# Eight more early expert tiles, two to a batch in the last eight routing batches

## The chip, the cores and the metric

The kernel runs on one core of a Trainium2 chip. The metric is the device time of one execution in microseconds (us); lower is better. A core has a matrix engine (TensorE, PE in the profile, with its weight loads as PEld), a vector engine (VectorE, DVE), a scalar engine (ScalarE, ACT), a general one (GpSimd, POOL) and one that here only issues transfers (SyncE, SP). Each engine works through its own list of instructions in order; semaphores tie the lists together.

## The reference

One transformer layer on 512 tokens of width 1024: a mixer (windowed attention beside a gated delta rule), then a PEER layer. In PEER every token picks, in each of 8 heads, 16 of 16,384 experts, by top-k over two lists of 128 sub-keys; each expert is one row of a table u and one of a table v:

```
out = einsum('tk,tkd->td', gelu(einsum('tkd,td->tk', u_tab[idx], x)) * gate, v_tab[idx])
```

## The kernel before

Tokens come in four blocks of 128. For blocks 1 to 3 (384 tokens) PEER is computed densely: the 16,384 experts form 128 tiles of 128 experts. "Up" multiplies a tile of u with the 384 tokens (24 matmuls of 128x384, since every operand is split into a high and a low part and three products are summed over 8 slices of the width), gelu follows, then a gate matrix that is zero where an expert was not picked, then "down" with the tile of v (18 matmuls of 128x512). For block 0 PEER is computed sparsely by "pairs": 128 picks, for each of which POOL gathers one row of u and v for every token (1 MB a gather, six slots), VectorE does one "dot" (L1528) and one "add" (L1545), and ScalarE a small gelu for each four dots (L1533). 128 dots and 128 adds are 256 steps of VectorE; `pair_steps` hands them out over the places of a list of rates, in groups of four dots, then four adds.

`routing` comes before `experts`. It picks the experts on VectorE and builds the gate matrix for the blocks b = 1, 2, 3, each in 16 batches k of 8 tokens. In a batch VectorE writes two one-hot tiles, oi (`first_keys`, one batch ahead) and oj; ScalarE scales oi to og (`gated`, eight instructions, L1798); TensorE multiplies og with oj (the products, L1762); ScalarE copies them out (L1814), and SP stores 1 MB of gates for each two batches. As TensorE has little to do there, routing also does the up step of some tiles ahead of time, the early tiles: 24 before the first batch and one in each of the 48 batches. An early tile n needs: a load of u by SP into one of four buffers; `split_u(n)` on ScalarE (L1776); `u_low(n)` on VectorE (L1665); the 24 matmuls of `up(n)` (L1734 to L1736); `gelu(n)` on ScalarE (L1783) into a single buffer, which is stored to memory (L1788, 192 KB) and read back in `experts`. `gelu(n)` waits until the store of n-1 has landed, and on ScalarE `split_u(n + 2)` stands right behind `gelu(n)`:

```
for n in early(b, k): gelu(n)        # evict(b, k): gelu(n), split_u(n + 2), store of n
```

In the order of the engines, for batch k of block 3:

- VectorE: oi(k+1), oj(k), `u_low` of the early tiles of batch k+1, the pair steps of batch k
- ScalarE: `gated(k)`, the pair gelu of the dots of batch k-1, `evict(k-1)` (the early tiles' gelu, split and store, then the copies of the products)
- TensorE: `up` of the early tiles of batch k, the products of batch k
- SP: the loads of u for the tiles four ahead, and after each odd batch a store of gates, which waits for `evict(k)`
- POOL: gathers for the pairs, as many as routing has dots; gather j waits for add j-6

`experts` then runs over the 128 tiles: the first NMT = 56 with both up and down, the other 72 with down alone, with the stored gelus. Its steps of the pairs go at 2.7 a tile in the first part and 1.0 in the second.

Of the kernel before, what the change touches and what calls it, by code (L numbers as in the profile page):

```python
# [12 lines left out]
P = 128  # L13
# [27 lines left out]
NK = 128  # L41
# [7 lines left out]
GT = 4  # L49
NG = NK // GT  # L50

EARLY = 72
NU = 4
TD = T - P
GRP4 = 4
# [1202 lines left out]
def output_projection(nc, m, ps, sem, w_out_in, early_u_in, u_t, norm_ffn_g, w_q, keys, h_dram):  # L1258
# [35 lines left out]
    with ExitStack() as ctx:  # L1294
# [14 lines left out]
        with nc.Block() as block:  # L1309
            @block.sync  # L1310
            def _(sp):
# [6 lines left out]
                for i in range(2):  # L1318
                    sp.dma_start(m.u_raw[i], u_t[NK - EARLY + i]).then_inc(early_u_in[i], 16)

# [237 lines left out]
def pair_steps(rates):  # L1558


    todo = [(what, GRP4 * g + i) for g in range(HA // GRP4) for what in ("dot", "add") for i in range(GRP4)]
    places, at, due = [], 0, 0.0
    for rate in rates:
        due += rate
        here = []
        while at < len(todo) and due >= 1.0:
            what, k = todo[at]
            if what == "add" and k % GRP4 == 0 and ("dot", k + GRP4 - 1) in here:
                break
            here.append(todo[at])  # L1570
            at, due = at + 1, due - 1.0
        places.append(here)
    places[-1] = places[-1] + todo[at:]
    return places


def routing(nc, m, ps, sem, u_in, next_u, u_t, gates, gelus, pairs_of_0, steps):
# [13 lines left out]
    NBT = P // BT  # L1591
    RING = 3
    ST = 16
    FIRST = 24
    AFTER = [()] + [tuple(range(NBT))] * (TB - 1)
    assert FIRST + sum(len(v) for v in AFTER) == EARLY

    def early(b, k):

        if b < 0:  # L1600
            return range(FIRST)
        n = FIRST + sum(len(v) for v in AFTER[:b]) + sum(i < k for i in AFTER[b])
        return range(n, n + (k in AFTER[b]))

    SMALL_AT = NBT - 2

    for n in early(-1, 0):
        banks.add(("up", n), "act")
    banks.add(("small", 1), "dve")
    for b in range(1, TB):  # L1610
        for k in range(NBT):
            for n in early(b, k):
                banks.add(("up", n), "act")
            for i in range(BT // 4):
                banks.add(("G", b, k, i), "act")
            if k == SMALL_AT and b + 1 < TB:
                banks.add(("small", b + 1), "dve")

    with ExitStack() as ctx:
# [47 lines left out]
        def slot(b, k):  # L1667
            return (NBT * (b - 1) + k) % RING

        def wait_products(eng, b, k):  # L1670

            n = NBT * (b - 1) + k - RING
            if n >= 0:
                banks.wait_full(eng, ("G", n // NBT + 1, n % NBT, BT // 4 - 1))

        with nc.Block() as block:
            @block.sync
            def _(sp):
                def load_u(n):

                    if n >= NU:
                        sp.wait_ge(u_lo, n - NU + 1)
                    sp.dma_start(u_raw[n % NU], u_t[NK - EARLY + n]).then_inc(u_in[n % NU], 16)

                for n in range(2, FIRST + NU):
                    load_u(n)
                for b in range(1, TB):
                    for k in range(NBT):
                        for n in early(b, k):
                            if n + NU < EARLY:  # L1690
                                load_u(n + NU)
                            else:
                                i = n + NU - EARLY
                                sp.wait_ge(u_lo, n + 1)
                                sp.dma_start(u_raw[i], u_t[i]).then_inc(next_u[i], 16)
                        if (k + 1) * BT % ST == 0:
                            q = ((k + 1) * BT // ST - 1) % 2
                            banks.wait_taken(sp, ("G", b, k, BT // 4 - 1))
                            t0 = (b - 1) * P + (k + 1) * BT - ST
                            sp.dma_start(gates[:, :, t0:t0 + ST, :].rearrange("g i t j -> i g (t j)"),  # L1700
                                         stage[:, q].rearrange("p g t j -> p g (t j)")).then_inc(stored[q], 16)
                for half in range(2):
                    sp.wait_ge(stored[half], 16 * (TD // ST // 2))
                sp.wait_ge(ge_out, 16 * EARLY)

# [63 lines left out]
            @block.scalar  # L1769
            def _(act):  # L1770
                def split_u(n):
                    act.wait_ge(u_in[n % NU], 16 * (n // NU + 1))
                    if n >= 2:

                        banks.wait_full(act, ("up", n - 2))
                    nc.scalar.activation(uh[:, n % 2, :], u_raw[n % NU], ACT.Copy).then_inc(u_hi, 1)  # L1776

                def gelu(n):

                    banks.wait_full(act, ("up", n))  # L1780
                    if n:
                        act.wait_ge(ge_out, 16 * n)
                    nc.scalar.activation(ge[:], banks.bank(("up", n))[:, 0:TD],  # L1783
                                         ACT.Gelu).then_inc(banks.taken["act"], 1)
                    if n + 2 < EARLY:
                        split_u(n + 2)
                    banks.wait_taken(act, ("up", n))
                    act.dma_start(gelus[n], ge[:]).then_inc(ge_out, 16)  # L1788

                def exps(b):  # L1790
                    act.wait_ge(subbed, b + 1)
                    nc.scalar.activation(best[:], best[:], ACT.Exp).then_inc(exped, 1)

                def gated(b, k):
                    act.wait_ge(oi_ready, NBT * (b - 1) + k + 1)
                    wait_products(act, b, k)
                    for t in range(BT):
                        ins = nc.scalar.activation(og[:, slot(b, k), t, :], oi[:, slot(b, k), t, :], ACT.Copy,  # L1798
                                                   scale=smallT[:, b % 2, 1, k * BT + t:k * BT + t + 1])
                        if t % 4 == 3:  # L1800
                            ins.then_inc(og_ready, 1)

                def evict(b, k):
                    for n in early(b, k):
                        gelu(n)
                    for i in range(BT // 4):
                        g = ("G", b, k, i)
                        banks.wait_full(act, g)
                        at = k * BT + 4 * i
                        half, q = (at // ST) % 2, (b - 1) * (P // ST) + at // ST  # L1810
                        if q >= 2 and at % ST == 0:
                            act.wait_ge(stored[half], 16 * (q // 2))
                        t0 = at % ST
                        nc.scalar.activation(stage[:, half, :, t0:t0 + 4, :].rearrange("p g t j -> p t g j"),  # L1814
                                             banks.bank(g)[:].rearrange("p (t g j) -> p t g j", t=4, j=GJ),
                                             ACT.Copy).then_inc(banks.taken["act"], 1)

                split_u(0)
                split_u(1)
                for n in early(-1, 0):  # L1820
                    gelu(n)
                    if n in (9, 20):
                        exps(n // 20)
                for b in range(1, TB):
                    for k in range(NBT):
                        gated(b, k)
                        if b == TB - 1 and k:
                            pairs_of_0.scalar_steps(act, steps[k - 1])
                        if k:
                            evict(b, k - 1)  # L1830
                        if k == 9 and b + 1 < TB:
                            exps(b + 1)
                    evict(b, NBT - 1)
                pairs_of_0.scalar_steps(act, steps[NBT - 1])
# [389 lines left out]
def hybrid_layer(nc, a, out):  # L2224
# [3 lines left out]
    with ExitStack() as ctx:  # L2228
# [55 lines left out]
        slots = [rows[:, i] for i in range(4)] + [more[:, i] for i in range(2)]  # L2284
        pairs_of_0 = Gathered(nc, sem, slots, m.mix[:, 0, :], mem.take("pair_index", [P, HA], U32)[:],
                              mem.take("pair_gate", [P, HA])[:], a["peer_uv"], mem.take)
        rates = [2.0] * (P // 8) + [2.7] * (NK - EARLY) + [1.0] * EARLY
        steps = pair_steps(rates)
        before, after = steps[:P // 8], steps[P // 8:]
        routing(nc, m, ps, sem, early_u_in, u_in, a["peer_u"], gates, gelus, pairs_of_0, before)  # L2290
        experts(nc, m, ps, sem, u_in, a["peer_u"], a["peer_v"], gates, gelus, h_dram, out, pairs_of_0, before, after)

# [23 lines left out]
```

## Time and profile before

| | us |
|---|---|
| median of 3 runs | 1674.74 |
| these runs | 1674.64 to 1679.88 |
| the profiled execution | 1674.7 |
| its span, first to last instruction | 1672.9 |

| engine | busy us | share of the span |
|---|---|---|
| TensorE | 1567.6 | 94% |
| VectorE | 1305.2 | 78% |
| ScalarE | 713.8 | 43% |
| GpSimd | 340.4 | 20% |

Times of rows count from the start of the span. Block 3 of the routing lies between 776 and 890 us, `experts` from 890 us to the end. In a row of the timeline the first number is the start, the second the duration, and what stands in brackets is the idle time of the engine before it and what ended that.

### The profile page before, as it was taken

How to read it: one execution, taken by the hardware profiler on the slowest of the kernel's cores; microseconds unless marked ns; L12 is line 12 of the kernel's file. 1: busy time of each engine (PE TensorE's matmuls, PEld its weight loads, DVE VectorE, ACT ScalarE, POOL GpSimd, SP SyncE). 2: the span in 40 equal slices, each digit the busy share in tenths (PEclk: the TensorE clock that was granted, in tenths of full speed). 3: DMA queues.
4: the chain of work that ended last, by engine and by line, in shares of the span. 5: the costliest groups of instructions: out<-in, count | busy, mean ns of one | idle time of the engine just before them, and what ended most of it. 6: DMA issues, size and time to landing. Idle time of an engine off the chain costs nothing. (4 is left out here: it accounts for less than half of the span.)

```text
span 1672.9 us, 24431 instructions
## 1 busy us (share of the span) xinstructions
PE 1567.6 (94%) x9241; PEld 1405.8 (84%) x9241; DVE 1305.2 (78%) x2270; ACT 713.8 (43%) x1411; POOL 340.4 (20%) x303
## 2 busy tenths in 40 slices
PE   7999787988899889989996999999999999999998
PEld 6898777767789889889995899999999988888886
DVE  4638775453499799998894988888798888998996
ACT  4645442132233668777672333333333333333331
POOL 5012710000165200020401221222222221100100
PEclk9999887988999999999998999999999999999999
DMA  5220003031144456686988988888898789999992
GB/s 191 76 76 8 2 2 132 22 139 63 56 156 157 148 157 194 205 302 213 358 278 342 407 315 316 324 317 314 323 364 293 275 345 382 368 363 345 352 339 90
DMA packets 147159, 380.89 MB, mean 228 GB/s; under 512 B 10480, under 2 KB 89456, under 8 KB 128368
## 3 DMA queue, kind: packets, MB, share of 16 engines
q1 hardware_dynamic: 118256, 231.17, 39.3%
q0 software_dynamic: 18432, 134.23, 20.6%
q10 hardware_dynamic: 10368, 14.16, 2.3%
q8 instruction: 60, 0.98, 0.2%
q14 instruction: 43, 0.35, 0.1%
HBM read 336.00 MB, written 43.52 MB: 227 GB/s over the span
## 5 line engine op out<-in xcount | busy, mean ns | idle before, releaser
L1521 POOL DMA_INDIRECT scores<-in_peer_uv,pair_index x86 | 123.6, 1437 | 626.6 <-DVE pair_sum L1545 462.7
L2114 PE MATMUL bank<-v_hi,act_hi 128*128 128x512 f32 x552 | 215.2, 390 | 5.0 <-DVE v_lo L2177 5.0
L2116 PE MATMUL bank<-v_hi,act_lo 128*128 128x512 f32 x552 | 219.3, 397 | 0.0
L2115 PE MATMUL bank<-v_lo,act_hi 128*128 128x512 f32 x552 | 216.4, 392 | 0.0
L1734 PE MATMUL bank<-x_hi,early_u_h 128*128 128x384 f32 x576 | 201.1, 349 | 16.3 <-POOL early_u_l L1665 11.5
L1735 PE MATMUL bank<-x_lo,early_u_h 128*128 128x384 f32 x576 | 196.9, 342 | 0.0
L1736 PE MATMUL bank<-x_hi,early_u_l 128*128 128x384 f32 x576 | 196.2, 341 | 0.0
L2190 DVE TENSOR_TENSOR act_tile<-gelu_tile,gate_tiles 128x384 f32<-128x384 f32 x128 | 119.7, 935 | 83.3 <-ACT gelu_tile L2162 71.0
L2102 PE MATMUL bank<-x_hi,u_split 128*128 128x384 f32 x448 | 151.6, 338 | 12.7 <-DVE u_split L2172 12.7
L2104 PE MATMUL bank<-x_hi,u_split 128*128 128x384 f32 x448 | 151.5, 338 | 0.0
L2103 PE MATMUL bank<-x_lo,u_split 128*128 128x384 f32 x448 | 151.5, 338 | 0.0
L1798 ACT ACTIVATE onehot_gated<-onehot_i,rt_smallT 128x128 f32<-128x128 f32 x384 | 117.8, 399 | 34.3 <-DVE onehot_i L1949 34.3
L2150 ACT ACTIVATE act_hi<-act_tile 128x384 fp32r<-128x384 f32 x128 | 66.8, 522 | 142.2 <-DVE act_tile L2190 122.7
L1734 PEld LDWEIGHTS bank<-x_hi,early_u_h 128*128 128x128 f32 x576 | 109.9, 191 | 20.8 <-POOL early_u_l L1665 6.7
L2114 PEld LDWEIGHTS bank<-v_hi,act_hi 128*128 128x128 f32 x552 | 103.8, 188 | 26.8 <-issue 6.2
L2162 ACT ACTIVATE gelu_tile<-bank 128x384 f32<-128x384 f32 x56 | 27.5, 491 | 228.1 <-PE bank L2104 228.0
L2115 PEld LDWEIGHTS bank<-v_lo,act_hi 128*128 128x128 f32 x552 | 103.7, 188 | 23.5
L2116 PEld LDWEIGHTS bank<-v_hi,act_lo 128*128 128x128 f32 x552 | 103.6, 188 | 22.5
L2177 DVE TENSOR_TENSOR v_lo<-v_raw,v_hi 128x1024 fp32r<-128x1024 f32 x92 | 112.3, 1220 | 9.9 <-ACT v_hi L2144 9.9
L2144 ACT ACTIVATE v_hi<-v_raw 128x1024 fp32r<-128x1024 f32 x92 | 96.7, 1051 | 33.8 <-DMA v_raw<-in_peer_v 31.7
L1762 PE MATMUL bank<-onehot_j,onehot_gated 128*128 128x128 f32 x768 | 96.2, 278 | 14.8 <-DVE onehot_j L1949 12.2
L1735 PEld LDWEIGHTS bank<-x_lo,early_u_h 128*128 128x128 f32 x576 | 110.0, 191 | 0.0
(327 smaller groups left out, 3674.7 us busy)
## 6 DMA issues: line engine op xcount, KB each, us to landing
v_raw<-in_peer_v SPq DMA_DIRECT2D x128, 512.0 KB, 6.5
u_raw<-in_peer_u SPq DMA_DIRECT2D x64, 512.0 KB, 6.3
u_raw_more<-in_peer_u SPq DMA_DIRECT2D x64, 512.0 KB, 6.0
gates<-gate_stage SPq DMA_DIRECT2D x24, 1024.0 KB, 5.8
gate_tiles<-gates SPq DMA_DIRECT2D x16, 1536.0 KB, 14.3
early_gelus<-early_gelu ACTq DMA_DIRECT2D x72, 192.0 KB
gelu_tile<-early_gelus SPq DMA_DIRECT2D x72, 192.0 KB, 7.7
w_raw<-in_w_in SPq DMA_DIRECT2D x9, 1024.0 KB, 5.3
```

Of the source, the lines that this page charges most:

```text
L1521: pool.indirect_dma_start(self.slot(k), None, self.table, bass.IndirectOffsetOnAxis(ap=self.sidx[:, k:k + 1], axis=0)).then_inc(self.lande ...
L1734: nc.tensor.matmul(banks.bank(g)[:, 0:TD], uh[:, q, w], m.xh[:, k, P:], start=(k == 0), stop=False)
L1735: nc.tensor.matmul(banks.bank(g)[:, 0:TD], uh[:, q, w], m.xl[:, k, P:], start=False, stop=False)
L1736: t = nc.tensor.matmul(banks.bank(g)[:, 0:TD], ul[:, q, w], m.xh[:, k, P:], start=False, stop=(k == KD - 1))
L1798: ins = nc.scalar.activation(og[:, slot(b, k), t, :], oi[:, slot(b, k), t, :], ACT.Copy, scale=smallT[:, b % 2, 1, k * BT + t:k * BT + t + 1])
L2102: nc.tensor.matmul(bank, uh[:, q, w], m.xh[:, k, P:], start=(k == 0), stop=False)
L2103: nc.tensor.matmul(bank, uh[:, q, w], m.xl[:, k, P:], start=False, stop=False)
L2104: t = nc.tensor.matmul(bank, ul[:, q, w], m.xh[:, k, P:], start=False, stop=(k == KD - 1))
L2114: nc.tensor.matmul(bank[:], ah[:, s, w], v_hi[:, c], start=first, stop=False)
L2115: nc.tensor.matmul(bank[:], ah[:, s, w], v_lo[:, c], start=False, stop=False)
L2116: t = nc.tensor.matmul(bank[:], al[:, s, w], v_hi[:, c], start=False, stop=last)
L2190: nc.vector.tensor_tensor(af[:], ge[:, n % NG2, :], gt[:, it % 2, :, jj], ALU.mult).then_inc(gate_f, 1)
```

## The change

`EARLY` goes from 72 to 80, so NMT goes from 56 to 48. In the batches 8 to 15 of block 3 there are two early tiles instead of one. The pair steps of these batches go from 2 to 4 a batch. On ScalarE `evict(k-1)` now stands ahead of the pair gelu of batch k-1.

```diff
-EARLY = 72
+EARLY = 80
...
     AFTER = [()] + [tuple(range(NBT))] * (TB - 1)
+    AFTER[-1] += tuple(range(NBT // 2, NBT))
...
-        return range(n, n + (k in AFTER[b]))
+        return range(n, n + AFTER[b].count(k))
...
                         gated(b, k)
+                        if k:
+                            evict(b, k - 1)
                         if b == TB - 1 and k:
                             pairs_of_0.scalar_steps(act, steps[k - 1])
-                        if k:
-                            evict(b, k - 1)
...
-        rates = [2.0] * (P // 8) + [2.7] * (NK - EARLY) + [1.0] * EARLY
+        rates = [2.0] * (P // 16) + [4.0] * (P // 16) + [2.7] * (NK - EARLY) + [1.0] * EARLY
```

## Rows read from the trace of the kernel before

**Rows 1.** Two stretches: length; busy PE, PEld, DVE, ACT, POOL; clock; DMA share; GB/s.

```profile
822.00:876.00 54.00, 51.29 (x330) 51.13 (x329) 46.92 (x52) 38.67 (x99) 10.28 (x6) 0.97 0.87 304
930.00:1340.00 410.00, 410.00 (x2070) 371.41 (x2069) 346.18 (x419) 142.86 (x216) 101.07 (x67) 1.00 0.85 323
```

**Rows 2.** The chain that ended last: start, us, what; same instruction, successive tiles.

```profile
954.65 0.24 PE bank L2116
962.98 0.24 PE bank L2116
...
1369.60 0.24 PE bank L2115
1386.19 0.24 PE bank L2115
```

**Rows 3.** Timeline of TensorE in block 3: the products of two successive batches.

```profile
847.96 1.95 PE L1762 MATMUL bank<-onehot_j,onehot_gated 128*128 128x128 f32 x16
...
853.97 1.95 PE L1762 MATMUL bank<-onehot_j,onehot_gated 128*128 128x128 f32 x16
```

**Rows 4.** Timeline of VectorE in block 3.

```profile
797.25 1.22 DVE L1949 TENSOR_TENSOR onehot_i<-rt_iota_row,rt_smallT 128x1024 f32<-128x1024 f32 x1
...
822.00 1.22 DVE L1949 TENSOR_TENSOR onehot_i<-rt_iota_row,rt_smallT 128x1024 f32<-128x1024 f32 x1
...
834.76 1.22 DVE L1665 TENSOR_TENSOR early_u_l<-u_raw,early_u_h 128x1024 fp32r<-128x1024 f32 x1 [4.27 <-ACT early_u_h L1776]
835.91 1.22 DVE L1528 SCALAR_TENSOR_TENSOR scores<-scores,mix 128x1024 f32<-128x1024 f32 x1
...
838.19 1.22 DVE L1949 TENSOR_TENSOR onehot_i<-rt_iota_row,rt_smallT 128x1024 f32<-128x1024 f32 x1
...
848.43 0.15 DVE L1539 TENSOR_TENSOR pair_c<-pair_g,pair_gate 128x4 f32<-128x4 f32 x1
...
851.01 1.22 DVE L1949 TENSOR_TENSOR onehot_i<-rt_iota_row,rt_smallT 128x1024 f32<-128x1024 f32 x1
...
875.94 1.22 DVE L1949 TENSOR_TENSOR onehot_j<-rt_iota_row,rt_smallT 128x1024 f32<-128x1024 f32 x1
```

**Rows 5.** Timeline of ScalarE: stores of early gelus and the gelus behind them.

```profile
536.05 0.33 ACTq L1788 DMA_DIRECT2D early_gelus<-early_gelu  x1
538.22 0.49 ACT L1783 ACTIVATE early_gelu<-bank 128x384 f32<-128x384 f32 x1 [1.25 <-PE bank L1736]
...
796.62 0.33 ACTq L1788 DMA_DIRECT2D early_gelus<-early_gelu  x1
...
798.50 2.47 ACT L1798 ACTIVATE onehot_gated<-onehot_i,rt_smallT 128x128 f32<-128x128 f32 x8
804.91 0.49 ACT L1783 ACTIVATE early_gelu<-bank 128x384 f32<-128x384 f32 x1 [3.95 <-DMA early_gelus<-early_gelu]
...
805.43 0.33 ACTq L1788 DMA_DIRECT2D early_gelus<-early_gelu  x1
...
809.90 0.49 ACT L1783 ACTIVATE early_gelu<-bank 128x384 f32<-128x384 f32 x1 [0.24 <-DMA early_gelus<-early_gelu]
...
823.65 0.33 ACTq L1788 DMA_DIRECT2D early_gelus<-early_gelu  x1
...
833.29 0.49 ACT L1783 ACTIVATE early_gelu<-bank 128x384 f32<-128x384 f32 x1 [5.42 <-DMA early_gelus<-early_gelu]
```

**Rows 6.** The groups by line of instructions: ScalarE's copies of the products, two a batch.

```profile
L1814 ACT ACTIVATE gate_stage<-bank 128x512 f32<-128x512 f32 x96 | 51.5, 592 | 0.9 <-ACT early_gelu L1783 0.9
```

**Rows 7.** Timeline of GpSimd: the last of four gathers.

```profile
829.34 1.96 POOL L1521 DMA_INDIRECT scores<-in_peer_uv,pair_index  x1 [0.30 <-issue]
```

**Rows 8.** Timeline of SP: loads of u, the last store of gates, the first load of experts.

```profile
819.66 3.76 SPq L1683 DMA_DIRECT2D u_raw_more<-in_peer_u  x2
...
884.71 0.38 SPq L1700 DMA_DIRECT2D gates<-gate_stage  x1
890.23 0.33 SPq L2053 DMA_DIRECT2D gate_tiles<-gates  x1
```

## The prediction

> **What bounds the kernel now.** I read the page first (TensorE busy in 94% of the span), then the busy time by stretch, then the chain of waits, then the timelines of TensorE, VectorE, ScalarE and SP around the last eight routing batches. The reader is to see two things. In `experts` TensorE has no idle time at all (410.00 of 410.00 us) [rows 1], and the chain that ended last is TensorE's alone: a tile with up and down takes 962.98 - 954.65 = 8.33 us, one with down alone (1386.19 - 1369.60) / 4 = 4.15 us [rows 2]. In the routing batches into which the tiles move, TensorE is nearly full as well: 51.29 of 54 us [rows 1], one batch each 853.97 - 847.96 = 6.01 us [rows 3]. So the change moves work of the bounding engine from one full stretch to another. What it can win at most is TensorE's idle time there, some 3 us in the stretch; what it can lose is whatever keeps TensorE waiting in the eight changed batches.
>
> **The change part by part.**
>
> *Experts.* Eight tiles lose their up step: 8 x (8.33 - 4.15) = -33.4 us [rows 2]. They gain a read of 192 KB each, and routing a store of as much, 3 MB in all. In experts reads lie under TensorE; if that cover were gone, 1.5 MB at 323 GB/s [rows 1] would be 5 us. The 16 pair steps that leave experts leave VectorE, which has slack there (346 of 410 us busy [rows 1]): nothing. The loads of u are as many as before.
>
> *TensorE in routing.* One up step is 8.33 - 4.15 = 4.18 us, so the products are 6.01 - 4.18 = 1.83 us and a batch with two up steps 10.2 us. Eight of them give the 33.4 us back exactly. If TensorE stayed the bound, the change would be worth nothing either way.
>
> *The handoff between ScalarE and VectorE.* This is where I see the cost. `split_u(n + 2)` stands behind `gelu(n)`. With one tile a batch, two tiles ahead are two batches ahead: `u_low` in VectorE's batch k needs only `evict(k-1)`, which follows `gated(k)`, whose oi was written in the batch before. With two tiles a batch, two tiles ahead are one batch ahead. VectorE's batch k needs `evict(k)`, which on ScalarE follows `gated(k+1)`, which needs oi(k+1), which VectorE writes at the start of that same batch k. So the engines take turns, once round in every batch, and the second `u_low` also waits for the second gelu, which waits for the store of the first to land. All of VectorE's pair steps stand behind that, and oi(k+2) behind them. (The old place of the pair gelu would even close a circle; that is why its move costs nothing but is needed. In the first eight batches it now stands some 1.3 us later, and the adds that wait for it have `u_low` before them.)
>
> The round, from the start of oi:
> - oi to the start of `gated`: 798.50 - 797.25 = 1.25 us; the eight scalings 2.4 us (2.47 in the row, of which the last overlaps) [rows 4, 5]. The first gelu starts at 3.6.
> - first gelu to second gelu: X, below.
> - gelu to `u_low` (through the split): 834.76 - 833.29 = 1.47; `u_low` 835.91 - 834.76 = 1.15 [rows 4, 5].
> - pair steps: two dots take 838.19 - 835.91 = 2.28, so four take 4.6; two adds with the small multiply take 851.01 - 848.43 = 2.58, so four take 5.0 [rows 4].
>
> That is 10.8 + X for a batch of dots and 11.2 + X for one of adds. The rounds are VectorE's batches 8 to 14, four of dots and three of adds: 4 x 10.8 + 3 x 11.2 = 76.8 us plus seven X.
>
> X is 0.5 us from gelu to the issue of its store, then the time until the next gelu may start. No row of before shows two gelus waiting in this way in these batches; the bounds are these [rows 5]. Below: 538.22 - 536.05 = 2.2 us, where the store wasn't what was waited for. Above: 833.29 - 823.65 = 9.6 us, right behind loads of u (issued until 823.4 [rows 8]) and among gathers, the last of them issued until 831.3 [rows 7]. Between: 8.3 us (804.91 - 796.62) and 4.5 us (809.90 - 805.43). In the changed batches the last load of u is released by the `u_low` of the round before, about 9 us ahead of the store, so it should be out of the way. The gathers are not: four follow the adds of batches 9 and 11 and two those of 7 and 13, and they run while the first gelu of batches 10, 12, 8 and 14 is stored. For these four I take 6.0 us, below the middle of 4.5 and 9.6 because the loads are gone; for the three others 2.2. With the 0.5: 4 x 6.5 + 3 x 2.7 = 34.1 us.
>
> The rounds together: 76.8 + 34.1 = 110.9 us, 15.8 a batch, against the 10.2 of TensorE, which now waits.
>
> Batch 7 is half such a round: its second `u_low` needs the gelu that before came at 833.29. VectorE's batch 7 began at 822.00 [rows 4]. If that gelu comes as late as before, it ends at 834.76 + 1.15 + 2.58 = 838.5, 16.5 us; with a short store ScalarE's own work (the store's issue at 823.65, copies of 2 x 0.6 [rows 6], `gated` at 2.5, in all some 4.2 us) puts the gelu near 827.9, `u_low` at 829.4 and the end 3.7 us later, 11.1 us in all. I take 13.8.
>
> Before, the same stretch of VectorE, oi in batch 7 to oj in batch 15, was 875.94 - 822.00 = 53.9 us [rows 4]. So: 110.9 + 13.8 - 53.9 = +70.8 us.
>
> *The end of routing.* From oj(15) to the first load of experts it took 890.23 - 875.94 = 14.3 us, 5.5 of it the last store of gates [rows 4, 8]. With two gelus there it is about 0.3 + X + 0.5 for the gelu + 1.1 for the copies [rows 6] + 0.4 + the same 5.5, so 10.5 at X = 2.7 and 14.3 at X = 6.5: I take -2, and 0 and -4 as ends.
>
> **Sum:** -33.4 + 70.8 - 2 = +35.4 us on 1674.7 us of the profiled execution, which is also the median of the runs: 1710 us.
>
> The Trainium skill speaks against one term, and for the first rival below. The Trainium skill (DMA: Bandwidth & Descriptors, section "Queues, rings and completion order") says that a DMA engine takes turns between the queues that have work. A 192 KB store would then share with two other queues, and at the 304 GB/s of this stretch the 0.38 MB of the others would add some 1.3 us to 2.2; by that estimate the four long waits are 3.5 us, not 6.0, and the time is 10 us shorter, 1700. The 9.6 and 8.3 us that the timeline shows speak against it.
>
> **The rivals.**
> - *Stores land fast even beside gathers.* All X = 2.7, batch 7 at 11.1, the end at -4: 76.8 + 18.9 + 11.1 - 53.9 - 4 - 33.4 = +15.5, so 1690. For it: the 4.5 us beside gathers. Against it: 8.3 and 9.6. This is the low end. 0.12.
> - *Stores land late everywhere*, 9.6 beside gathers and 4.5 elsewhere: 4 x 10.1 + 3 x 5.0 = 55.4; with 16.5 and 0 that is 76.8 + 55.4 + 16.5 - 53.9 - 33.4 = +61.4, so 1736. 0.05.
> - *TensorE falls to the lower of its two clock levels* (1.2 in place of 2.4 GHz), since it now idles some 5 us in a batch, in pieces. At half the clock a batch of TensorE takes up to 2 x 10.2 = 20.4 us, over the 15.8 of the round; if it stayed there for all seven, +32 us, 1742; for half of them 1726. For it: every batch has such gaps. Against it: the mean of 0.97 in this stretch [rows 1] in spite of the wait behind the 9.6 us store, so it came back soon. Short falls cost nothing, as TensorE isn't the bound. 0.08.
> - *The other side: TensorE stays the bound.* If the turns overlap, because some split comes a batch earlier than I read, a batch is 10.2 us, and the two 33.4 cancel. The time is 1669 to 1676, the low end if the 4.27 us stall of VectorE in the stretch [rows 4] goes. It decides as soon as the round is under 10.2 us, which even with X = 0 it isn't by the order of the instructions (10.8). 0.07.
>
> **How the numbers follow.** The forecast has 0.68, with a range of its own of 1697 to 1727. A measurement of this kernel tells about 0.3%, 5 us, from no change. All cases but the last are slower: 0.93; the last gives 0.05 within and 0.02 faster. The range from 1690 to 1733 reaches to the low rival and to a clock that is low for most of the rounds; it leaves out the last rival, the late stores and the edges of the others, under 2 in 10.
>
> **What would show it.** In the changed kernel: `early_u_l` on VectorE waiting for `early_u_h` some 3 us and again X us in each of the batches 8 to 14; the products of these batches 13 to 19 us apart and uneven, longer after batches of adds; TensorE waiting for `early_u_l`; the gelus of second tiles waiting for the store; experts at 8.33 and 4.15 us a tile, 33.4 us shorter. Products 10.2 us apart would prove me wrong on the turns; waits that alternate otherwise, on the stores.

## The result, and the profile after

The changed kernel takes 1721.85 us (median of 4, 1718.95 to 1728.51) against 1675.68 us (median of 4): a ratio of 1.0276, 95% interval 1.0241 to 1.0312. It is slower, 46 us by the medians, where +35 (1710 us) was forecast; 1721.85 lies in the range of 1690 to 1733. The profiled execution took 1718.95 us with a span of 1717.2, 44.3 us more than the 1672.9 of before. One of the eleven runs of e10 below, the profiled one, took 2579.5 us at a mean granted clock of 0.56 where the others took 1661 to 1674, and no reading rests on it. From here on "round" means the time from one oi(k+1) to the next on VectorE, counted by batch k.

First the busy time by stretch of the changed kernel (length; then busy us of PE, PEld, DVE, ACT and POOL, with instructions; granted clock; DMA share; GB/s): the stretch of [rows 1], then rounds 8 and 9 by themselves, then experts.

```profile
822.00:876.00 54.00, 40.27 (x233) 37.94 (x232) 30.21 (x31) 23.62 (x56) 12.79 (x8) 0.94 0.77 268
834.14:854.61 20.47, 13.03 (x68) 12.27 (x67) 9.31 (x12) 6.18 (x14) 2.86 (x2) 0.83 0.78 278
854.61:868.25 13.64, 11.07 (x68) 10.59 (x67) 9.67 (x12) 6.38 (x15) 2.67 (x2) 1.00 0.38 107
1000.00:1300.00 300.00, 299.75 (x1514) 271.35 (x1513) 253.10 (x307) 103.61 (x156) 79.04 (x49) 1.00 0.85 325
```

In experts TensorE is as full as before once it has started. In the routing stretch TensorE is busy 40.27 of 54 us where it was 51.29 [rows 1]. VectorE, 30.21, isn't full either: no engine is. That is what engines look like that take turns. VectorE's timeline shows the turns (start, us, instruction, idle time before it):

```profile
834.14 1.22 DVE L1950 TENSOR_TENSOR onehot_i<-rt_iota_row,rt_smallT 128x1024 f32<-128x1024 f32 x1
...
839.20 1.23 DVE L1666 TENSOR_TENSOR early_u_l<-u_raw_more,early_u_h 128x1024 fp32r<-128x1024 f32 x1 [2.70 <-ACT early_u_h L1777]
848.89 1.22 DVE L1666 TENSOR_TENSOR early_u_l<-u_raw_more,early_u_h 128x1024 fp32r<-128x1024 f32 x1 [8.46 <-ACT early_u_h L1777]
...
854.61 1.22 DVE L1950 TENSOR_TENSOR onehot_i<-rt_iota_row,rt_smallT 128x1024 f32<-128x1024 f32 x1
...
859.66 1.22 DVE L1666 TENSOR_TENSOR early_u_l<-u_raw,early_u_h 128x1024 fp32r<-128x1024 f32 x1 [2.70 <-ACT early_u_h L1777]
862.12 1.23 DVE L1666 TENSOR_TENSOR early_u_l<-u_raw,early_u_h 128x1024 fp32r<-128x1024 f32 x1 [1.23 <-ACT early_u_h L1777]
...
868.25 1.22 DVE L1950 TENSOR_TENSOR onehot_i<-rt_iota_row,rt_smallT 128x1024 f32<-128x1024 f32 x1
...
952.35 1.22 DVE L1950 TENSOR_TENSOR onehot_j<-rt_iota_row,rt_smallT 128x1024 f32<-128x1024 f32 x1
```

Where [rows 4] had one wait of 4.27 us in eight batches (the others of that stretch are 1.1 us or less), each round now has two: 2.70 us for the first split, the same in all rounds, and then one for the second split, 8.46 us in round 8 and 1.23 in round 9. ScalarE's timeline shows what the second one is, the gelu behind a store [rows 5]:

```profile
838.25 0.33 ACTq L1789 DMA_DIRECT2D early_gelus<-early_gelu  x1
847.42 0.49 ACT L1784 ACTIVATE early_gelu<-bank 128x384 f32<-128x384 f32 x1 [8.26 <-DMA early_gelus<-early_gelu]
...
858.72 0.33 ACTq L1789 DMA_DIRECT2D early_gelus<-early_gelu  x1
...
860.65 0.49 ACT L1784 ACTIVATE early_gelu<-bank 128x384 f32<-128x384 f32 x1 [1.02 <-DMA early_gelus<-early_gelu]
```

From the issue of the store to the next gelu it is 9.17 us in round 8 and 1.93 in round 9. The rounds 8 to 14 are 20.47, 13.64, 19.49, 13.64, 18.94, 13.64 and 18.39 us; the sum is 118.2. The accounts of the two spans, from the starts of oi and oj and from SP's first load of experts (SP's timeline, [rows 8]):

```profile
957.03 0.38 SPq L1701 DMA_DIRECT2D gates<-gate_stage  x1
962.55 0.33 SPq L2054 DMA_DIRECT2D gate_tiles<-gates  x1
```

| stretch | before us | after us | difference | forecast |
|---|---|---|---|---|
| up to oi of batch 7 | 822.00 | 822.63 | +0.6 | 0 |
| batch 7 and the rounds 8 to 14 | 53.94 | 129.72 | +75.8 | +70.8 |
| oj(15) to experts | 14.29 | 10.20 | -4.1 | -2 |
| experts | 782.67 | 754.65 | -28.0 | -33.4 |
| span | 1672.9 | 1717.2 | +44.3 | +35.4 |

### The profile page after: what moved, and what is told of

Its sections match the earlier page's. It is cut to its first block and busy times, and to the rows that moved or that the text cites. A ratio compares the mean times of both kernels' runs of the same rounds, so it can differ in the third digit from the quotient of the medians.

```text
span 1717.2 us, 24437 instructions
## 1 busy us (share of the span) xinstructions
PE 1578.3 (92%) x9241; PEld 1411.5 (82%) x9241; DVE 1308.7 (76%) x2270; ACT 712.3 (41%) x1411; POOL 338.9 (20%) x303
## 5 line engine op out<-in xcount | busy, mean ns | idle before, releaser
L1735 PE MATMUL bank<-x_hi,early_u_h 128*128 128x384 f32 x640 | 226.2, 353 | 44.8 <-DVE early_u_l L1666 32.8
L1736 PE MATMUL bank<-x_lo,early_u_h 128*128 128x384 f32 x640 | 221.4, 346 | 0.0
L1737 PE MATMUL bank<-x_hi,early_u_l 128*128 128x384 f32 x640 | 220.5, 345 | 0.0
L1735 PEld LDWEIGHTS bank<-x_hi,early_u_h 128*128 128x128 f32 x640 | 124.6, 195 | 51.8 <-issue 22.0
L2103 PE MATMUL bank<-x_hi,u_split 128*128 128x384 f32 x384 | 130.1, 339 | 9.3 <-DVE u_split L2173 9.3
L2105 PE MATMUL bank<-x_hi,u_split 128*128 128x384 f32 x384 | 130.0, 338 | 0.0
L2104 PE MATMUL bank<-x_lo,u_split 128*128 128x384 f32 x384 | 129.8, 338 | 0.0
L1736 PEld LDWEIGHTS bank<-x_lo,early_u_h 128*128 128x128 f32 x640 | 124.4, 194 | 0.0
L1737 PEld LDWEIGHTS bank<-x_hi,early_u_l 128*128 128x128 f32 x640 | 124.1, 194 | 0.0
L1763 PEld LDWEIGHTS bank<-onehot_j,onehot_gated 128*128 128x128 f32 x768 | 92.6, 194 | 26.7 <-DVE onehot_j L1950 25.0
L1545 DVE SCALAR_TENSOR_TENSOR pair_sum<-scores,pair_c,pair_sum 128x1024 f32<-128x1024 f32 x86 | 107.1, 1280 | 0.7
```

The source lines that it names most:

```text
L1545: self.nc.vector.scalar_tensor_tensor(total, self.slot(k)[:, D:], self.c[:, at:at + 1], total, ALU.mult, ALU.add).then_inc(self.summed, 1)
L1735: nc.tensor.matmul(banks.bank(g)[:, 0:TD], uh[:, q, w], m.xh[:, k, P:], start=(k == 0), stop=False)
L1736: nc.tensor.matmul(banks.bank(g)[:, 0:TD], uh[:, q, w], m.xl[:, k, P:], start=False, stop=False)
L1737: t = nc.tensor.matmul(banks.bank(g)[:, 0:TD], ul[:, q, w], m.xh[:, k, P:], start=False, stop=(k == KD - 1))
L1763: t = nc.tensor.matmul(banks.bank(g)[:, q * NK:(q + 1) * NK], og[:, slot(b, k), 4 * i + q, :], oj[:, slot(b, k), 4 * i + q, :], start=True ...
L2103: nc.tensor.matmul(bank, uh[:, q, w], m.xh[:, k, P:], start=(k == 0), stop=False)
```

## The experiments

Ten kernels ran. Each was timed beside the kernel before, and the ratio is to that; e1, e2 and e3 rest on two runs each, e4 on three, the others on nine to eleven. Spans, stretches and rounds are those of one profiled execution each. Two theories were open at first: the engines take turns, with the long waits due to the gathers of the pairs (mine), or something simpler: the doubled pair steps, or the loads of u that SP issues just behind a store.

**Hold the loads of u (e1).** In the changed kernel's rounds 8, 10, 12 and 14 SP issues a load some 2 us behind the store (840.45 in round 8); in the others it is held by its store of gates. That is a second reason for the same pattern.

```diff
                         for n in early(b, k):
+                            if b == TB - 1 and k >= NBT // 2:
+                                sp.wait_ge(ge_out, 16 * (n - 1))
                             if n + NU < EARLY:
```

> The changed kernel, but in its last eight routing batches SP holds the load of u for tile n+4 until the store of the early gelu n-2 has landed. So no load of u is issued while a store is on its way. Theory (engines take turns; the stores of the rounds 8, 10, 12, 14 are late because of the gathers of the pairs): the wait between the two gelus of these rounds stays at 7.5 to 9.7 us, the rounds stay at 18 to 20 us, the time within 5 us of the changed kernel's 1722. Rival (the load of u that SP issues some 2 us behind the store is what delays it; in the rounds 9, 11, 13 SP is still held by its store of gates, so nothing competes there): all waits fall to 2.4 us, all rounds to 13.5 us, the time to about 1697.

Measured: 1718.27 us against 1677.3, ratio 1.0245 (1.0198 to 1.0291). The rounds are 20.27, 13.63, 19.12, 13.63, 18.43, 13.64 and 17.97. Round 10 on ScalarE, and SP beside it:

```profile
873.52 0.33 ACTq L1791 DMA_DIRECT2D early_gelus<-early_gelu  x1
881.34 0.49 ACT L1786 ACTIVATE early_gelu<-bank 128x384 f32<-128x384 f32 x1 [6.91 <-DMA early_gelus<-early_gelu]
```
```profile
864.73 2.82 SPq L1684 DMA_DIRECT2D u_raw<-in_peer_u  x2
881.27 5.63 SPq L1684 DMA_DIRECT2D u_raw_more<-in_peer_u  x2
```

No load is issued between 867.6 and 881.3, and the next gelu still comes 7.8 us after the store is issued. The loads are worth some 0.4 us in each long round, not 6. The rival fell.

**Shift the pairs (e2).** The batches of dots and adds change places; the stores of gates stay.

```diff
-        rates = [2.0] * (P // 16) + [4.0] * (P // 16) + [2.7] * (NK - EARLY) + [1.0] * EARLY
+        rates = [2.0] * (P // 16) + [0.0] + [4.0] * (P // 16 - 1) + [2.8] * (NK - EARLY) + [1.0] * EARLY
```

> The changed kernel, but with no pair step in routing batch 8 and four from batch 9 on, so that batches of dots and of adds change places (dots in 9, 11, 13, 15, adds in 10, 12, 14) against the stores of gates, which stay where they are; the steps left over go to experts (2.8 instead of 2.7 a tile). Theory (gathers follow the adds and delay the first store of the next round): the long waits between two gelus are in the rounds 8 (gathers after the adds of batch 7), 11 and 13, the short ones of 2.4 us in 9, 10, 12 and 14; rounds of 13.5 and 19 us, round 8 some 16; the sum some 11 us less than in the changed kernel, the end of routing some 5 us longer, the time 1713 to 1720. Rival (SP's order of loads and stores of gates sets it): long waits stay in 8, 10, 12, 14.

Measured: 1706.85 us, ratio 1.0176 (1.0091 to 1.0262). The rounds 8 to 14 are 16.80, 14.27, 13.65, 18.80, 13.63, 18.76 and 13.64. Round 8 has no pair step, so its 16.80 hold a wait too (10.1 us from the store to the next gelu); the waits are long in 8, 11 and 13, as the gathers say. Round 11 on ScalarE, GpSimd and SP:

```profile
883.69 0.33 ACTq L1789 DMA_DIRECT2D early_gelus<-early_gelu  x1
891.20 0.49 ACT L1784 ACTIVATE early_gelu<-bank 128x384 f32<-128x384 f32 x1 [6.59 <-DMA early_gelus<-early_gelu]
```
```profile
876.35 1.74 POOL L1521 DMA_INDIRECT scores<-in_peer_uv,pair_index  x1 [38.32 <-DVE pair_sum L1545]
878.40 0.94 POOL L1521 DMA_INDIRECT scores<-in_peer_uv,pair_index  x1 [0.30 <-issue]
879.64 1.98 POOL L1521 DMA_INDIRECT pair_rows<-in_peer_uv,pair_index  x1 [0.30 <-issue]
881.92 0.94 POOL L1521 DMA_INDIRECT pair_rows<-in_peer_uv,pair_index  x1 [0.31 <-issue]
```
```profile
872.25 2.79 SPq L1684 DMA_DIRECT2D u_raw_more<-in_peer_u  x2
893.63 0.38 SPq L1701 DMA_DIRECT2D gates<-gate_stage  x1
```

SP issued nothing for 18 us; four gathers of 1 MB were issued just ahead of the store. Round 10 of the same kernel is the counterpart, on SP and ScalarE:

```profile
861.19 0.38 SPq L1701 DMA_DIRECT2D gates<-gate_stage  x1
861.61 2.88 SPq L1684 DMA_DIRECT2D u_raw<-in_peer_u  x2
```
```profile
870.05 0.33 ACTq L1789 DMA_DIRECT2D early_gelus<-early_gelu  x1
871.99 0.49 ACT L1784 ACTIVATE early_gelu<-bank 128x384 f32<-128x384 f32 x1 [1.03 <-DMA early_gelus<-early_gelu]
```

Its store of gates and its loads of u come as far ahead of the store of the gelu as in round 10 of the changed kernel (863.1 to 866.4 there, the store at 872.35), but there are no gathers, and the next gelu follows 1.94 us behind the issue where it was 8.20. So the long wait follows the gathers. The median of the two runs (1701.26 and 1712.43) is 6 us below what I expected. In the profiled one, the faster, experts was short (745.2 us), and the end of routing took 9.8 us against 10.2, where I had expected 5 more.

**Tiles only (e3)** and **steps only (e4)**. The changed kernel with two pair steps in each batch, and the kernel before with four in the last eight; e4 keeps the changed order on ScalarE.

```diff
-        rates = [2.0] * (P // 16) + [4.0] * (P // 16) + [2.7] * (NK - EARLY) + [1.0] * EARLY
+        rates = [2.0] * (P // 8) + [3.05] * (NK - EARLY) + [1.0] * EARLY
```
```diff
-EARLY = 80
+EARLY = 72
-    AFTER[-1] += tuple(range(NBT // 2, NBT))
```

> The changed kernel with two pair steps in every batch of the last routing block, as in the kernel before, and 3.05 instead of 2.7 a tile in the first part of experts, so that all are done. Theory (engines take turns because two tiles a batch leave one batch of lookahead): rounds of 8.5 to 8.8 us plus the wait between gelus, so 11 us where it is short (9, 10, 13, 14) and 16 to 18 where it is long (8, 11, 12: two gathers each), sum 96 us against 118, the time about 1698, still some 23 over the kernel before. Rival (the doubled pair steps on VectorE are what costs): back to 1675 to 1680.

> The kernel before (72 early tiles, one a batch) with four pair steps a batch in the last eight routing batches and the pair gelu behind the early gelu, as in the changed one. Theory: lookahead stays two batches, no turns; VectorE alone bounds the batches, 3 x 1.15 + 4.6 or 5.0 = 8.1 to 8.5 us each, 66 us for eight against 54, the time about 1687; VectorE waits for splits only when a store is late. Rival (the doubled steps are what costs): 1710 or more.

Measured: e3 1696.05 us, ratio 1.0112 (1.0027 to 1.0197); e4 1689.99 us, ratio 1.0071 (1.0048 to 1.0094). In e3 the rounds are 10.96 to 18.47, with the same first wait; their sum is 90.7 us where I had 96, as gathers come only ahead of rounds 8 and 11, and the wait of VectorE in 11 is no longer than 4.08 us. In e4 they are 8.0 to 12.2, and the first wait is gone: the only wait for a split in these rounds is 4.07 us in round 8, for a late store, as in [rows 4]. The first low part of a round on VectorE, of e3 and of e4:

```profile
879.11 1.23 DVE L1666 TENSOR_TENSOR early_u_l<-u_raw_more,early_u_h 128x1024 fp32r<-128x1024 f32 x1 [2.71 <-ACT early_u_h L1777]
```
```profile
860.31 1.22 DVE L1949 TENSOR_TENSOR onehot_j<-rt_iota_row,rt_smallT 128x1024 f32<-128x1024 f32 x1
861.45 1.22 DVE L1665 TENSOR_TENSOR early_u_l<-u_raw,early_u_h 128x1024 fp32r<-128x1024 f32 x1
```

The wait belongs to two tiles a batch, not to the steps. Each half of the change costs something alone, 19 and 12 us by the ratios, the 19 from two runs 11 us apart. Whether both together (46) cost more than the sum isn't shown: by the spans of the profiled executions it is 26.9 + 16.3 us against 44.3. In the rounds 8 to 14 there is a difference: their sum is 47.8 us before, 90.7 in e3, 64.1 in e4 and 118.2 with both, 11 us more than the two halves add. It isn't the steps: without the time from gelu to gelu the rounds of e3 take 60.3 us and those of the changed kernel 76.8, the same 16 us that the steps cost in e4. It is the stores: the seven times from gelu to gelu sum to 30.4 us in e3, with gathers ahead of two of the stores, and to 41.4 in the changed kernel, with gathers ahead of four.

**Two gelu buffers (e5), pair steps first (e6), both (e7).**

```diff
-        ge = sb("early_gelu", [P, TD])
+        ge = sb("early_gelu", [P, 2, TD])
...
-                    if n:
-                        act.wait_ge(ge_out, 16 * n)
+                    if n >= 2:
+                        act.wait_ge(ge_out[n % 2], 16 * (n // 2))
```
```diff
+                        if b + 1 == TB:
+                            pairs_of_0.vector_steps(dve, steps[k])
                         for n in early_next(b, k):
                             dve.wait_ge(u_hi, n + 1)
                             u_low(nc.vector, n).then_inc(u_lo, 1)
...
-                        if b + 1 == TB:
-                            pairs_of_0.vector_steps(dve, steps[k])
```

> The changed kernel with two buffers for the early gelus and a semaphore for each, so that a gelu waits for the store of the gelu before the last one. Theory: the second gelu of a round follows the first one's split, 1.4 us behind the first; all rounds become 10.8 or 11.2 + 1.4, so 12.3 to 12.6 us, sum 87 against 118, the time about 1689. What is left against the kernel before is the turns. Rival (stores are not what stretches the rounds): no change from 1722.

> The changed kernel, but in the last block VectorE does the pair steps of a batch ahead of the low parts of the next tiles, so that they run while ScalarE scales, does the gelus and waits for the store; one buffer still. Theory: a round is then 3.6 + X + 1.5 + 1.15 us, at least TensorE's 10.2: 10.2 with a short wait X, 14 to 15 with a long one; sum about 90 against 118, the time about 1690. Rival (the steps weren't in the ring): no change.

> Both of the last two edits on the changed kernel: two buffers and pair steps first. Theory: the ring of turns takes 9.2 us or less, under TensorE's 10.2, so TensorE bounds all rounds; sum 72 us; eight of them cost what experts gives back, and the time is that of the kernel before within 5 us, 1670 to 1677. Rival (TensorE's low clock or contention keeps a cost): over 1685.

| kernel | median us (10 runs) | ratio to before | rounds 8 to 14 us | their sum |
|---|---|---|---|---|
| e5 | 1681.56 | 1.0002 (0.9975 to 1.0030) | 12.1 to 12.5 | 86.4 |
| e6 | 1687.10 | 1.0049 (1.0027 to 1.0071) | 9.5 and 13.3 to 15.0 | 85.0 |
| e7 | 1665.86 | 0.9933 (0.9910 to 0.9957) | 10.2 | 71.6 |

The kernel before had 1679.79 us in these runs. Of the 118.2 us of the rounds either edit alone takes 32 or 33, both together 47: in a ring, steps and waits partly stand in for each other. In e5 the second wait is gone (0.40 us in round 8, none behind it) and the first stands as it was; both low parts run together (VectorE's timeline):

```profile
871.19 2.54 DVE L1666 TENSOR_TENSOR early_u_l<-u_raw,early_u_h 128x1024 fp32r<-128x1024 f32 x2 [2.70 <-ACT early_u_h L1778]
```

In e7 TensorE is the bound (its timeline, and busy time in columns as above):

```profile
840.75 1.95 PE L1764 MATMUL bank<-onehot_j,onehot_gated 128*128 128x128 f32 x16
850.97 1.95 PE L1764 MATMUL bank<-onehot_j,onehot_gated 128*128 128x128 f32 x16
861.19 1.95 PE L1764 MATMUL bank<-onehot_j,onehot_gated 128*128 128x128 f32 x16
```
```profile
815.00:895.00 80.00, 80.00 (x508) 79.97 (x507) 72.97 (x82) 50.90 (x117) 17.87 (x13) 1.00 1.03 383
```

10.22 us apart, busy 80.00 of 80. This is the rival "TensorE stays the bound", made real. Two expectations missed by time, not by rounds: e5 came in 7 us and e7 at least 4 us lower than expected. I had left out the batches 0 to 6 of the block. From its first oi to batch 7 the changed kernel takes 59.4 us, e5 and e7 take 52.9 and 53.9.

**The kernel before with the same edits (e8, e10), and oi two batches ahead (e9).** e8 is the kernel before with two gelu buffers, e10 also with the pair steps first; e9 is e5 with `first_keys` one batch earlier:

```diff
                     first_keys(b, 0)
+                    first_keys(b, 1)
                     for k in range(NBT):
-                        if k + 1 < NBT:
-                            first_keys(b, k + 1)
+                        if k + 2 < NBT:
+                            first_keys(b, k + 2)
```

> The kernel before with two buffers for the early gelus. Theory: stores are on its path only where one is late (one stall of 4.3 us on VectorE in the last eight batches, and the end of routing, where the last gelu waited 5.3 us for the store before it): 4 to 9 us less, 1667 to 1671. Rival (they are hidden): 1675.

> The kernel before (72 early tiles) with two gelu buffers and the pair steps ahead of the low parts. Theory: with one tile a batch there are two batches of lookahead and nothing to gain from the order; TensorE bounds the batches at 6.0 us with two buffers already; the same as two buffers alone and as 80 tiles with both edits, 1665 to 1669. Rival (80 tiles have an advantage of their own, hidden until both edits are made): 80 tiles with both edits are faster than this by 3 us or more.

> The changed kernel with two gelu buffers, and with VectorE writing oi two batches ahead instead of one. The second wait of the turn (for the store) is already gone; this takes away the first, from oi through the scaling to the first gelu. Theory: a round that follows a batch of dots still has ScalarE waiting for the dots (pair gelu), then scaling, so 11.5 us; one that follows adds has its scaling done during the adds, so TensorE's 10.2; the 2.7 us wait of VectorE for the first split goes in these. Sum of seven about 76 us against the 86 of two buffers alone, the time some 10 us less than that kernel, about 1671. Rival (the rounds with two buffers are set by VectorE's own work or TensorE): no change from two buffers alone, 1681.

Measured: e8 1667.3 us, ratio 0.9920 (0.9892 to 0.9948), its batches 5.8 to 6.6 us. e10 1665.92 us, ratio 0.9927 (0.9902 to 0.9953); of e10 only the times are used. e7, e8 and e10 can't be told apart: with the stores out of the way, 72 and 80 tiles are worth the same. By the profiled executions of e7 and e8, batch 7 and the rounds cost 79.98 - 48.36 = 31.6 us more with 80 tiles, and experts 785.33 - 754.41 = 30.9 us less.

e9 took 1679.33 us, ratio 1.0006 (0.9979 to 1.0033): no gain on e5, where I had expected 10 us. The first wait did shrink, to 1.66 us behind batches of dots and to nothing behind adds, but the dots now had to wait for their gather (VectorE's timeline):

```profile
863.53 1.23 DVE L1528 SCALAR_TENSOR_TENSOR scores<-scores,mix 128x1024 f32<-128x1024 f32 x1 [2.75 <-DMA scores<-in_peer_uv,pair_index]
...
868.69 2.54 DVE L1666 TENSOR_TENSOR early_u_l<-u_raw,early_u_h 128x1024 fp32r<-128x1024 f32 x2 [1.66 <-ACT early_u_h L1778]
```

Such a wait, 2.5 to 2.8 us, stands in batches 10, 12 and 14, and in the batches of dots there are 0.6 to 3.0 us for the second split as well. I read it as another ring at about 12 us a round: adds free slots, gathers fill them, dots wait for these; no run tests this reading. So the expectation failed, and the rival got the time right. But VectorE was busy for 65.1 of the 85.6 us from oi(10) to oj(15) and TensorE for 80.8, at a mean clock of 0.96: nearly full, but with idle time left.

## Why the prediction was right, point by point

- **TensorE's work only moves.** Right. e7 shows 10.22 us a batch (10.2 forecast), and gives back in experts, to within 1 us, what it costs in routing.
- **The turns.** Right, and shown by edits: the first wait is 2.70 us in every round, absent with one tile a batch (e4), and the sum of rounds falls from 118.2 to 85.0 when the steps run inside the wait (e6). Without X a round of dots was forecast at 10.8 us and measures 20.47 - 9.67 = 10.80; one of adds 11.2, and 13.64 - 2.43 = 11.21. The wholly direct test, two batches of lookahead with twice the split buffers, was not made. That the move of the pair gelu is needed was read from the order of the instructions; no run has two tiles a batch with the pair gelu in its old place.
- **The store's wait X.** The mechanism and the four rounds were right, the size was off: this is the term of the sum that was mis-sized. The three short ones were forecast at 2.7 and are 2.43 to 2.45 us. The four long ones were forecast at 6.5 and are 9.67, 8.70, 8.14 and 7.60: 34.1 against 26.0, so 8.1 us of the miss. I had taken less than the middle of the rows because the loads of u would be out of the way. Those ahead of the store were. Two more are issued 2.2 us behind it, released by the first `u_low` of the same round, which I had not seen, but e1 shows that they hardly matter, and e2 that the gathers are enough. The Trainium skill (DMA: Bandwidth & Descriptors, section "Queues, rings and completion order") says that the DMA engines take turns between queues; the 3.5 us estimated from it for these waits is not borne out by the 7.1 to 9.2 us measured from the issue to the next gelu, and the measurement decides. The estimate had taken the turns for equal shares of bytes; what fails is the estimate, and no run here tests the turns themselves.
- **Batch 7** took 11.51 us (13.8 forecast, between 11.1 and 16.5), and **the end of routing** gave -4.1 (-2 forecast, -4 as its end).
- **Experts.** Forecast -33.4, in this execution -28.0. Over the eight profiled kernels with 80 tiles it is 745.2 to 754.7 us, mean 751.8, over the three with 72 it is 782.7 to 785.3, mean 784.3: -32.6, so the term stands to within 1 us. Most of the 5.4 us missing in this execution is a late transfer some ten tiles into the down-only part, on the chain that ended last (in order of time; below it the row of TensorE's timeline):

```profile
1387.81 19.39 DMA v_raw<-in_peer_v
1407.23 1.06 ACT v_hi_late L2145
1408.31 1.24 DVE v_lo_late L2178
```
```profile
1409.69 0.47 PE L2115 MATMUL bank<-v_hi_late,act_hi 128*128 128x512 f32 x1 [3.34 <-DVE v_lo_late L2178]
```

TensorE waited 3.34 us, and matmuls behind it ran 0.43 us apart instead of 0.23 up to 1413.9, some 1.5 us more. It needn't be chance: TensorE waits 1.2 to 3.6 us for this tile in six of the eight kernels with 80 tiles and in none of the three with 72. Why isn't known.

- **The clock.** The granted clock fell and came back (0.83 in the mean of round 8, 1.00 in round 9) and wasn't the bound, as expected: round 11, with a mean of 0.86, took the same 13.64 us as round 9.

The miss of the profiled span adds up: X +8.1 in the long and -0.8 in the short rounds, batch 7 -2.3, the end -2.1, experts +5.4, the start +0.6, together +8.9 on +35.4. The terms missed by 14.1 us upward and by 5.2 downward, and that these partly cancel is luck.

## What to carry to other kernels

Lookahead counted in items shrinks when a loop body handles more of them: two buffers were two batches at one tile a batch and one batch at two, and then in-order engines wait for each other in every batch though none is full. Before moving work of the bounding engine, ask whether the place it goes to has idle time of that engine; here it had 3 us. And a single buffer that waits for its store to land is harmless only as long as nobody waits for the next use: the second buffer was worth 0.8% to the kernel before.

## What the runs showed of the hardware

A 192 KB store on ScalarE's queue took 1.9 us from its issue to the next gelu in the rounds with no gather or load issued beside it. When two or four 1 MB gathers of GpSimd had been issued ahead of it, it took 7.1 to 9.2 us in the changed kernel, 6.7 to 9.0 with no load issued behind it (e1), 7.5 to 10.1 in e2, and 4.8 and 9.5 in e3 behind two gathers. The number of gathers doesn't order these times: 9.17 and 7.10 us in rounds 8 and 14, with two, 8.20 and 7.64 in rounds 10 and 12, with four. What the DMA engines did meanwhile is in the last two columns, for the waits of rounds 10 and 9 (columns as in [rows 1]):

```profile
872.35:880.55 8.20, 4.80 (x28) 4.32 (x26) 1.23 (x1) 0.92 (x2) 0.00 (x0) 1.00 1.01 409
858.72:860.65 1.93, 0.35 (x4) 0.16 (x2) 0.98 (x1) 0.91 (x1) 0.00 (x0) 1.00 0.28 102
```

TensorE's granted clock fell to its lower level, 0.50, behind an idle time of 5.25 us in round 8 (TensorE's timeline, and the stretch from there):

```profile
850.26 0.66 PE L1735 MATMUL bank<-x_hi,early_u_h 128*128 128x384 f32 x1 [5.25 <-DVE early_u_l L1666]
```
```profile
850.26:852.00 1.74, 1.74 (x6) 1.74 (x7) 1.74 (x3) 0.00 (x0) 0.00 (x0) 0.50 0.49 122
```

The first matmul took 0.66 us there, and also behind 4.27 and 3.81 us in rounds 10 and 12; behind 3.17 us in round 14 and 1.97 in round 8 it took 0.41. From 854.61 on the granted clock was 1.00 again.
